# Attention scores that alternate between the partition halves, and probabilities scaled on GpSimd

## The reference

```
scores = einsum('bnqhgd,bnkhd->bnhgqk', qb, kw) * scale     # a block of 128 queries, its own and the previous 128 keys
scores = where(valid, scores, -1e30)                        # band of 128; the first block has no previous keys
probs  = softmax(concatenate([scores, sink], -1))[..., :-1]
out    = einsum('bnhgqk,bnkhd->bnqhgd', probs, vw)
return out.reshape(B, S, Q_DIM) @ w_o + b_o
```

## Time and profile before

| | |
|---|---|
| median of 3 runs | 1924.72 us (1924.55 to 1925.39) |
| span of the profiled execution | 1923.7 us |
| TensorE busy | 1903.5 us (99%) |
| VectorE busy | 1020.8 us (53%) |
| ScalarE busy | 628.1 us (33%) |
| GpSimd busy | 4.2 us |
| mean granted TensorE clock | 0.999 |

### The profile page before, as it was taken

The page is one execution under the profiler, slowest core; times in us unless marked ns, Lnnn a source line. Parts: engine busy times, 40 slices in busy tenths (PEclk is TensorE's granted clock), DMA queues, the critical chain, the costliest instruction groups (busy, mean ns, idle before and its releaser), DMA issues.

```text
span 1923.7 us, 24217 instructions
## 1 busy us (share of the span) xinstructions
PE 1903.5 (99%) x8977; PEld 1557.3 (81%) x8989; DVE 1020.8 (53%) x1393; ACT 628.1 (33%) x911; POOL 4.2 (0%) x13
## 2 busy tenths in 40 slices
PE   8999999999999999999999999999999999999998
PEld 6888888777687888888888888887898878888886
DVE  5434434677847434434764344457765674344345
ACT  5322222444534312223442232234112542222223
POOL 0000000000000000000000000000000000000000
PEclk9999999999999999999999999999999999999999
DMA  5332322321022232232333323232433223333231
GB/s 193 107 107 88 100 97 98 110 77 44 1 88 81 94 99 98 98 98 88 99 99 98 98 91 106 88 111 77 126 121 95 77 70 106 98 96 91 97 98 55
DMA packets 60849, 180.90 MB, mean 94 GB/s; under 512 B 6144, under 2 KB 15504, under 8 KB 60784
## 3 DMA queue, kind: packets, MB, share of 16 engines
q1 hardware_dynamic: 60432, 179.09, 28.8%
q0 software_dynamic: 352, 0.92, 0.1%
HBM read 173.69 MB, written 6.29 MB: 94 GB/s over the span
## 4 chain that ended last, share of the span: by engine, by line
PE 97%; DVE 1%; ACT 1%; DMA 0%; issue 0%; SPq 0%; DVEq 0%; ACTq 0%
PE bank L340 27%; PE bank L341 26%; PE bank L342 26%; PE bank L652 3%; PE bank L379 2%; PE bank L380 2%; PE bank L383 2%; PE bank L562 2%; PE bank L357 1%; PE bank L601 1%; PE bank L583 1%; PE bank L537 1%; PE bank L660 1%; PE bank L515 0%; DVE w_lo L966 0%; ACT w_hi L741 0%
## 5 line engine op out<-in xcount | busy, mean ns | idle before, releaser
L966 DVE TENSOR_TENSOR w_lo<-w_raw,w_hi 128x1024 fp32r<-128x1024 f32 x312 | 381.6, 1225 | 455.8 <-ACT w_hi L741 445.3
L340 PE MATMUL bank<-x_hi,w_hi 128*128 128x512 f32 x1448 | 569.7, 393 | 0.8 <-DVE gate_tmp L999 0.2
L342 PE MATMUL bank<-x_hi,w_lo 128*128 128x512 f32 x1448 | 563.6, 389 | 0.0
L341 PE MATMUL bank<-x_lo,w_hi 128*128 128x512 f32 x1448 | 563.4, 389 | 0.0
L741 ACT ACTIVATE w_hi<-w_raw 128x1024 fp32r<-128x1024 f32 x312 | 328.2, 1055 | 613.8 <-PE bank L342 609.5
L340 PEld LDWEIGHTS bank<-x_hi,w_hi 128*128 128x128 f32 x1448 | 271.9, 188 | 61.6 <-issue 3.8
L340 PE MATMUL bank<-a_hi,w_hi 128*128 128x512 f32 (+1 forms) x844 | 320.7, 380 | 0.4 <-DVE w_lo L966 0.4
L341 PE MATMUL bank<-a_lo,w_hi 128*128 128x512 f32 (+1 forms) x844 | 320.0, 379 | 0.0
L342 PE MATMUL bank<-a_hi,w_lo 128*128 128x512 f32 (+1 forms) x844 | 319.9, 379 | 0.0
L341 PEld LDWEIGHTS bank<-x_lo,w_hi 128*128 128x128 f32 x1448 | 271.9, 188 | 57.9 <-issue 2.6
L342 PEld LDWEIGHTS bank<-x_hi,w_lo 128*128 128x128 f32 x1448 | 271.8, 188 | 56.8
(11 more groups left out here) (166 smaller groups left out, 1282.9 us busy)
## 6 DMA issues: line engine op xcount, KB each, us to landing
w_raw<-stream SPq DMA_DIRECT2D x312, 512.0 KB, 3.4
h_resid<-xT SPq DMA_DIRECT2D x8, 256.0 KB, 6.2
w_raw<-stream SPq DMA_DIRECT2D x8, 256.0 KB, 5.9
u_scratch<-V SPq DMA_DIRECT2D x8, 256.0 KB, 2.0
u_groups<-u_scratch SPq DMA_DIRECT2D x8, 256.0 KB, 2.8
qT<-z_scratch SPq DMA_DIRECT2D x8, 256.0 KB, 3.7
outT<-h_resid SPq DMA_DIRECT2D x8, 256.0 KB, 2.2
z_scratch<-kT SPq DMA_DIRECT2D x4, 256.0 KB, 2.3
```

The costliest lines, as they stand in the source:

```text
L340: nc.tensor.matmul(out, lw[0], lx[0], start=first, stop=False)
L341: nc.tensor.matmul(out, lw[0], lx[1], start=False, stop=False)
L342: return nc.tensor.matmul(out, lw[1], lx[0], start=False, stop=last)
L966: nc.vector.tensor_tensor(w_lo[:, s, :], raw[:, s, :], w_hi[:, s, :].bitcast(F32), ALU.subtract).then_inc(s_lo, 1)
```

## The change

`scores` issues both mask products first, then the four score products in the order half 0, half 1, half 0, half 1. `normalise` on VectorE keeps the sum and the reciprocal, in one of two halves of `den`, and signals a new semaphore `s_den`. GpSimd waits for it and multiplies the four heads' probabilities in place, as VectorE did before, and signals `s_p`. Before it writes `den` again, VectorE waits for the probabilities of step `t - 2`.

```diff
-        row_sum, den = sb("row_sum", [P, 2, 4]), sb("den", [P, 4])
+        row_sum, den = sb("row_sum", [P, 2, 4]), sb("den", [P, 2, 4])
...
+        s_den = sem("row_inverse_ready")
...
+            for t in range(4 * NB):
+                pool.wait_ge(s_den, t + 1)
+                for j in range(4):
+                    at = slice(2 * P - keys(t // 4), 2 * P)
+                    ins = nc.gpsimd.tensor_scalar(prob[t % 2][:, j, at], prob[t % 2][:, j, at],
+                                                  den[:, t % 2, j:j + 1], None, ALU.mult)
+                ins.then_inc(s_p, 1)
...
                 for b in range(2):
-                    out = bank[(4, 0)[t % 2] + b]
-                    nc.tensor.matmul(scored(out, n), ident_b[:, :], mask[:, :, 2 * P - keys(n):],
+                    nc.tensor.matmul(scored(bank[(4, 0)[t % 2] + b], n), ident_b[:, :], mask[:, :, 2 * P - keys(n):],
                                      start=True, stop=False)
-                    for cc in range(2):
+                for cc in range(2):
+                    for b in range(2):
                         c, half = 2 * cp + cc, slice(b * HD, (b + 1) * HD)
-                        last = nc.tensor.matmul(scored(out, n)[:, cc, :],
+                        last = nc.tensor.matmul(scored(bank[(4, 0)[t % 2] + b], n)[:, cc, :],
...
                 dve.wait_ge(s_exp, t + 1)
-                link(nc.vector.tensor_tensor(den[:, :], row_sum[:, i, :], sink_e[:, i, :], ALU.add))
-                link(nc.vector.reciprocal(den[:, :], den[:, :]))
-                for j in range(4):
-                    at = slice(2 * P - keys(t // 4), 2 * P)
-                    ins = nc.vector.tensor_scalar(prob[i][:, j, at], prob[i][:, j, at], den[:, j:j + 1], None,
-                                                  ALU.mult)
-                ins.then_inc(s_p, 1)
+                if t >= 2:
+                    dve.wait_ge(s_p, t - 1)
+                link(nc.vector.tensor_tensor(den[:, i, :], row_sum[:, i, :], sink_e[:, i, :], ALU.add))
+                nc.vector.reciprocal(den[:, i, :], den[:, i, :]).then_inc(s_den, 1)
```

## The result

The changed kernel takes 1942.41 us (median of 4 runs, 1941.53 to 1944.26) against 1924.63 before: ratio 1.0095, 95% interval 1.0083 to 1.0107. It is slower by 18 us, where 1919.1 was forecast, and lies above the range. The profiled execution ran 1942.29 with a span of 1940.5.

The account below looks back on a forecast made before the run. TensorE's 4.70 us per full attention step was taken as the bound. Terms -1.5, +0.3, -1.8, -3.15 and +0.5 sum to -5.65 from a 1923.7 span, so 1918.0; with 1.0 for the runs' median, 1919.1, range 1910.5 to 1935.

Parts of the forecast that it names:

- TensorE sets the pace before, and the scores fall from 2.75 to 1.60: Full attention steps: TensorE fills the 4.70 us period; with paired halves the scores cost 1.15 us less on it.
- scores(0) and scores(1), -1.5: Score sets in the QKV stage, 128 keys: each falls from 1.71 to 0.96 us, 1.5 less for both, all on the path.
- The chain 2.35 + 4x: Full step: transposes, copy, sum and reciprocal, hand-overs and four GpSimd multiplications of x us each; 4.35 us forecast against 4.70.
- The price x = 0.50: Time in us of one GpSimd multiplication of 256 columns; each 0.1 on it is worth 4.8 us.
- The 0.41: Estimate of x: the memset's 0.144 us wholly fixed, plus 256 columns at VectorE's reduction slope of 1.05 ns.
- The upper bound of 1.15: Highest x in us: all of GpSimd's 32-column memset counted by the column, 0.144 x 8.
- No loss of clock: TensorE rests up to 0.8 us in each 4.35 us step and was taken to lose no clock from it.
- the steps behind 14 covered: Attention steps after step 14: covered by twelve WO products in front of each, so 0 us change.
- GpSimd setting a slower pace: Rival: the chain VectorE sum, GpSimd, transposes decides from x = 0.70; 1934 at x 0.8, 1953 at 1.15; chance 0.16.
- part 1: The new order of the score products, alternating between halves: 1.15 us less on TensorE in a full step.
- The two engines shutting each other out: Rival: VectorE holds GpSimd off for a whole reduction, up to 1.29 us a step, about 1935; chance 0.05.
- the small case: Only small VectorE instructions with two SBUF inputs collide with GpSimd's, each waiting at most one x, mostly off the chain: +0 to 1.

Follow-up runs that it names:

- one TENSOR_TENSOR of 1.89: The changed kernel with one GpSimd TENSOR_TENSOR over all four heads instead of its four TENSOR_SCALARs: 1917.06 us, ratio 0.9958.
- the two variants: The changed kernel with GpSimd's four TENSOR_SCALARs multiplying by a constant 0.5 (1936.61 us), or replaced by four TENSOR_TENSORs of 256 columns (1922.06 us).
- the idle products: The changed kernel with eight idle products before the transposes of full steps 4 to 13, in TensorE's wait for GpSimd: 1940.26 us, ratio 1.0077.
- three multiplications of VectorE and one of GpSimd: The changed kernel with GpSimd multiplying one head of four and VectorE the other three, both by TENSOR_SCALARs: 1918.47 us, ratio 0.9965.

## Why the prediction was wrong, point by point

- **TensorE sets the pace before, and the scores fall from 2.75 to 1.60**: right, 1.59 in the trace. The forecast's reason, that the halves pair like the V products, was right as well; that they must alternate for it was not part of the sum, and is not so.
- **scores(0) and scores(1), -1.5**: right in size, but not in what it brings. Set against VectorE's last slot before them (452.20 before, 453.09 after), the evacuation of V (461.08 and 460.49) comes 1.48 earlier, and the transposes of step 0 (462.60 and 462.15) 1.34. Those of step 1 (465.81 and 466.66) come only 0.04 earlier, as they wait for GpSimd (1.53 of idle time), where 1.5 less 0.3 was forecast: the same price x took it.
- **The chain 2.35 + 4x**: right, over a wide span. With x = 0.907 it gives 5.98 and the trace 5.94; with one TENSOR_TENSOR of 1.89, 4.24 and 4.19; with 3.30 and 2.32 in the two variants 5.65 and 4.67, for 5.60 and 4.63.
- **The price x = 0.50**: this is the step that failed, a mis-sized term. It measured 0.907 for 256 columns and 0.59 for 128, which is 0.27 fixed and 2.5 ns a column. The rows of the memset and of VectorE's reduction could not show it; I had put the value near the low end on the grounds that a memset is mostly fixed cost. The 0.41 borrowed VectorE's 1.05 ns a column, and the 0.50 taken in its place leaves 1.39 over the memset's 0.144, where 2.5 and a fixed 0.27 were measured. The upper bound of 1.15 did hold it, but the range stopped at 0.8. By the prediction's own 4.8 us for each 0.1, 0.907 gives 1919.1 + 19.5 = 1938.6.
- **No loss of clock, and the steps behind 14 covered**: both wrong and small, 1.4 to 2 us and 1.25 us. With them 1938.6 becomes 1941.2 to 1941.9, for 1942.41 measured. (1.4 is what the trace shows for the clock, 2 the difference that the idle products made.)
- **The rival that came true** is GpSimd setting a slower pace, given 0.16. Its deciding point, x = 0.70, was not run, but runs on both sides of it agree with it: 1922.06 at 0.58 and 1936.61 at 0.82. The change loses because it bought 1.15 us of TensorE and replaced 1.14 us of VectorE by 3.63 of GpSimd, on a chain of 5.94 that is longer than the old cover too. The cover that part 1 took away did not decide it: with the scores in their old order the loss is as large (1944.57).
- **The two engines shutting each other out**: in the changed kernel it is the small case. VectorE's reductions from PSUM (1.29) are as before beside GpSimd, and a small instruction suffers (L1165, mostly 0.34 instead of 0.17), off the chain. VectorE's copy (0.69) falls where GpSimd is idle and says nothing on this. The small instructions with two SBUF inputs, which the prediction had collide, take 0.16 and 0.15 as before in most steps, and up to 0.37 in a few. With VectorE multiplying in SBUF as well the engines do hold each other off, and a multiplication of 0.35 becomes one of 1.23. The Trainium skill, SBUF — State Buffer, Who interferes with whom, says that VectorE and GpSimd hold a shared port pair as a lock for whole instructions, and that a reduction does not take it. The traces agree on the reduction, and on the lock beside a TENSOR_TENSOR of GpSimd (1.23 beside 1.04). Beside its TENSOR_SCALAR they do not: three multiplications of VectorE and one of GpSimd were done in 1.29, where turns would need 1.78.
- **The page's price**: the estimate from the Trainium skill, GPSIMD Engine Reference, Elementwise side-by-side cycle accounting (1.5 ns a column for one input, more for two) differs from the measurement in both: TENSOR_SCALAR costs 2.5 ns a column, TENSOR_TENSOR (1.89 - 1.03) / 512 = 1.68 ns. The measurement decides.

## What to carry to other kernels

When two edits are made together, write down the chain that each leaves: the one through the new engine would have been harmless under 4.70 us of TensorE only if it were shorter than that, and the saving on TensorE could show no further than that chain. The two parts run singly (1918.79 and 1944.57) tell at once which of them loses. Work moved to an engine that has no row of its kind is a bet on one number; measure it first, and in more than one form. Products that use different halves of the array gain when no full-array product stands between them, in whatever order they come.

## What the runs showed of the hardware that was not expected

- GpSimd multiplies faster by TENSOR_TENSOR with a broadcast second input than by TENSOR_SCALAR, though it reads two tensors: 0.58 against 0.91 us for 128x256, 1.89 for 128x1024 in one instruction against 3.63 for the same work in four TENSOR_SCALARs.
- TensorE ran score products of two row halves, issued half by half, four instructions at a time (8 in 1.12 us), as it did with column halves.
- A VectorE multiplication in SBUF beside one of GpSimd depends on GpSimd's form: three took 1.29 instead of 0.86 beside a TENSOR_SCALAR of 1.08, and one took 1.23 instead of 0.35 beside a TENSOR_TENSOR of 1.04.
- A rest of 1.5 to 2.8 us of TensorE was in some steps followed by slow products (V products 1.75 instead of 1.09, score products 2.08 instead of 1.13), in others not. Of the nine full steps of the changed kernel four had slow products. The rests before its transposes from step 4 to step 13 were 2.80, 0.81, 2.36, 2.36, 1.52, 2.36, 0.78, 2.36, 2.36 and 1.31, and the slow products came in the steps behind the first, fourth, sixth and ninth of them. Idle products in the rest made all steps alike. Which rests cost the clock stays open.
